# Gates, norms and reciprocal rows moved into the delta steps; operand turns mixed into the first output tile

## The reference

```
h = rms_norm(x); proj = h @ w_in                 # q k v z of the delta net; q k v z of the window attention
dn = gated_deltanet_bidir(...)                   # forward and backward, chunks of 64 tokens, 4 heads of 128
dn = rms_norm(dn, dn_out_norm_w) * silu(dn_z)    # norm over each head's 128 values
sw = windowed_gqa_with_sinks(...) * silu(sw_z)   # 8 query heads of 64, window 128; softmax with a sink
x = x + concat(dn, sw) @ w_out
```

## Time and profile before

| | us |
|---|---|
| median of 3 runs | 2268.99 (2260.82 to 2269.74) |
| profiled execution | 2262.73 |
| its span | 2260.9 |
| TensorE busy in it | 2146.4 (95%) |
| VectorE busy | 1160.1 (51%) |
| ScalarE busy | 728.3 (32%) |
| GpSimd busy | 364.8 (16%) |
| mean granted clock of TensorE | 0.98 |

### The profile page before, as it was taken

The page is one execution under the profiler, slowest core; times in us unless marked ns, Lnnn a source line. Parts: engine busy times, 40 slices in busy tenths (PEclk is TensorE's granted clock), DMA queues, the critical chain, the costliest instruction groups (busy, mean ns, idle before and its releaser), DMA issues. The chain is left out here.

```text
span 2260.9 us, 33793 instructions
## 1 busy us (share of the span) xinstructions
PE 2146.4 (95%) x14358; PEld 1652.8 (73%) x14386; DVE 1160.1 (51%) x1716; ACT 728.3 (32%) x1272; POOL 364.8 (16%) x298
## 2 busy tenths in 40 slices
PE   7999998899987999999997898999999999999998
PEld 6888875677665777876764555778888878878887
DVE  6773326666765866644424665464433433442443
ACT  4223314333332352222224664353312222221221
POOL 3000004212324641111201221350000000000000
PEclk9999998999997999999998999999999999999999
DMA  5113321000004648311214002221111111111112
GB/s 211 47 47 102 92 89 68 2 2 2 2 2 187 203 147 311 126 39 56 76 47 173 1 1 94 79 71 47 44 50 56 41 45 56 47 40 54 47 33 98
DMA packets 185961, 165.81 MB, mean 73 GB/s; under 512 B 13440, under 2 KB 163796, under 8 KB 185684
## 3 DMA queue, kind: packets, MB, share of 16 engines
q1 hardware_dynamic: 180046, 145.18, 20.2%
q0 software_dynamic: 4784, 17.83, 2.0%
q10 hardware_dynamic: 982, 0.65, 0.1%
HBM read 136.90 MB, written 26.74 MB: 72 GB/s over the span
## 5 line engine op out<-in xcount | busy, mean ns | idle before, releaser
L250 PE MATMUL mix_acc<-mix_hi,w_hi 128*128 128x512 f32 x1040 | 415.8, 400 | 0.0
L252 PE MATMUL mix_acc<-mix_hi,w_lo 128*128 128x512 f32 x1040 | 409.9, 394 | 0.0
L251 PE MATMUL mix_acc<-m_lo,w_hi 128*128 128x512 f32 x1040 | 409.4, 394 | 0.0
L230 ACT ACTIVATE w_hi<-w_stage 128x1024 fp32r<-128x1024 f32 x154 | 162.6, 1056 | 457.7 <-PE mix_acc L252 249.1
L238 DVE TENSOR_TENSOR w_lo<-w_stage,w_hi 128x1024 fp32r<-128x1024 f32 x154 | 193.1, 1254 | 110.5 <-ACT w_hi L230 110.5
L3127 DVE SCALAR_TENSOR_TENSOR hidden<-mix_acc,hidden_conv,hidden 128x1023 f32<-128x1023 f32 x88 | 112.8, 1282 | 263.3 <-ACT hidden L3076 261.7
L250 PEld LDWEIGHTS mix_acc<-mix_hi,w_hi 128*128 128x128 f32 x1040 | 195.6, 188 | 52.2 <-issue 8.2
L252 PEld LDWEIGHTS mix_acc<-mix_hi,w_lo 128*128 128x128 f32 x1040 | 195.7, 188 | 45.9
L251 PEld LDWEIGHTS mix_acc<-m_lo,w_hi 128*128 128x128 f32 x1040 | 195.9, 188 | 43.4
L250 PE MATMUL acc<-h_hi,w_hi 128*128 128x512 f32 x400 | 156.8, 392 | 0.9 <-issue 0.9
L252 PE MATMUL acc<-h_hi,w_lo 128*128 128x512 f32 x400 | 155.8, 390 | 0.0
(11 more groups left out here) (359 smaller groups left out, 3741.4 us busy)
## 6 DMA issues: line engine op xcount, KB each, us to landing
w_stage<-in_w_in SPq DMA_DIRECT2D x48, 512.0 KB, 4.3
w_stage<-in_w_up SPq DMA_DIRECT2D x44, 512.0 KB, 3.7
w_stage<-in_w_out SPq DMA_DIRECT2D x32, 512.0 KB, 4.0
w_ada<-in_w_ada SPq DMA_DIRECT2D x32, 512.0 KB, 4.8
spill<-y_tok POOLq DMA_DIRECT2D x21, 512.0 KB, 5.1
m_resid<-resid_spill SPq DMA_DIRECT2D x2, 4096.0 KB, 16.2
conv_in<-in_w_ada SPq DMA_DIRECT2D x16, 512.0 KB, 6.0
conv_in<-spill SPq DMA_DIRECT2D x3, 2048.0 KB, 12.6
```

Of the source, the lines that this page charges most:

```text
L230: nc.scalar.activation(w_hi[:, slot], w_stage[:, slot], ACT.Copy).then_inc(w_hi_ready, 1)
L250: nc.tensor.matmul(acc[:, h, :], w_hi[:, slot, k, :], hi[:, k, tok], start=k == 0, stop=False)
L251: nc.tensor.matmul(acc[:, h, :], w_hi[:, slot, k, :], lo[:, k, tok], start=False, stop=False)
L252: mm = nc.tensor.matmul(acc[:, h, :], w_lo[:, slot, k, :], hi[:, k, tok], start=False, stop=k == kts - 1)
```

## The change

1. In the delta block SyncE loads the attention's gates one block of 128 rows at a time into the queries' place, once the block's scores are made; GpSimd multiplies them into `y_ch` in steps 7, 10, 13 and 15. Only the delta net's gates are loaded at the block's end, in two halves of the tokens.
2. Tiles 3 and 4 of the delta net are complete in step 11, tiles 2 and 5 in 13, tiles 1 and 6 in 15. Their squares (ACT, level 3) and sums (DVE, level 4) stand in that step, root (ACT, level 1) and scaling (DVE, levels 2 and 3) in the next.
3. In step 16 TensorE turns `rcp` at level 3 and ScalarE copies the rows.
4. In the first output projection only tile 0 is normed ahead of the products and tile 7 beside them, by GpSimd's scaling at step 1. The head's roots share one tile.
5. In both projections five units are turned first; units 5, 6 and 7 are turned ahead of the first tile's operands 1, 2 and 3.

```
+                for b in range(4):
+                    sp.wait_ge(s_sc, TT * b + TT)
+                    sp.wait_ge(s_wconst, 48 + 16 * b)
+                    sp.dma_start(qk[:, b, :], scratch(SP_SWZ + b)).then_inc(s_wconst, 16)
...
-                for i, first, signal in ((1, SP_SWZ, s_wconst), (0, SP_Z, s_zl)):
-                    sp.dma_start(conv_in[:, 4 * i:4 * i + 4, :],
+                for h, signal in enumerate((s_zl, s_qk)):
+                    cols = slice(h * HALF, (h + 1) * HALF)
+                    sp.dma_start(conv_in[:, 0:4, cols],
...
+        COMPLETE = {11: (3, 4), 13: (2, 5), 15: (1, 6)}
+        GATED_AT = {7: 0, 10: 1, 13: 2, 15: 3}
...
+                def gated(b):
+
+                    pool.wait_ge(s_wconst, 64 + 16 * b)
+                    pool.wait_ge(s_oc, TT * b + TT)
+                    nc.gpsimd.tensor_tensor(y_ch[:, b, :], y_ch[:, b, :], qk[:, b, :], ALU.mult).then_inc(mix_yn, 1)
...
+                        if s == NCH and lv == 3:
+                            pe.wait_ge(s_den, 4)
+                            for i in range(TT):
+                                mm = nc.tensor.transpose(scb[0:SW_HEADS, i // 4, i % 4 * P:(i % 4 + 1) * P], rcp[:, i, :],
+                                                         ident)
+                            mm.then_inc(s_mod, 1)
...
+                        if s - 1 in COMPLETE and lv == 1:
+                            roots(s - 1)
+                        if s in COMPLETE and lv == 3:
+                            squares(s)
+                        if s == NCH and lv == 3:
+                            copy_rows()
...
+                        if s in COMPLETE and lv == 4:
+                            out_sums(s)
+                        if s - 1 in COMPLETE and lv in (2, 3):
+                            outs_scaled(s - 1, lv - 2)
                         if 0 < s < NCH and lv == 4:
                             advance(s - 1, 0)
...
-            EARLY = 0 if windowed else 3
+            EARLY, TURNED_FIRST = 0 if windowed else 3, 5
...
+                for g in range(EARLY, TURNED_FIRST):
                     turn_unit(pe, g)
+
+                def first_ready(u):
+
+                    if TURNED_FIRST <= u + TURNED_FIRST - 1 < KT:
+                        turn_unit(pe, u + TURNED_FIRST - 1)
+                    pe.wait_ge(mix_lo, r * STEPS + u + 1)
...
+                for g in range(0 if windowed else EARLY - 1, KT):
+                    if windowed and g == 4:
+                        dve.wait_ge(*gates_loaded)
                     operand(dve, g)
-                for g in range(4 if windowed else EARLY - 1, KT):
-                    operand(dve, g)
+                    if windowed and g == 0:
+                        out_sum(0, 7)
+                    if windowed and g == 1:
+                        dve.wait_ge(mix_ors, 4)
+                        out_normed(nc.vector.tensor_tensor, 0)
```

More of the change, by code:

```diff
@@ L1346, in in_gap, with squares, roots, copy_rows @@
                         copy_out(u)
+                def squares(s):
+                    n, _ = completed(s)
+                    act.wait_ge(s_o, 2 * s - 2)
+                    act.wait_ge(mix_oss, 2 * n)
+                    act.wait_ge(mix_yn, 1)
+                    for j, i in enumerate(COMPLETE[s]):
+                        nc.scalar.activation(out_squares_of[:, j, :], o_dn[:, i, :], ACT.Square).then_inc(mix_osq, 1)
+                def roots(s):
+                    n, tiles = completed(s)
+                    act.wait_ge(mix_oss, 2 * n + 2)
+                    nc.scalar.activation(out_rs1[:, tiles, :], out_ss1[:, tiles, :], ACT.Ln, bias=eps[:, 0:1], scale=1.0 / P
+                                         ).then_inc(mix_ln, 1)
+                    act.wait_ge(mix_ln, n + 1)
+                    nc.scalar.activation(out_rs1[:, tiles, :], out_rs1[:, tiles, :], ACT.Exp, scale=-0.5
+                                         ).then_inc(mix_ors, 1)
+                def copy_rows():
+                    act.wait_ge(s_mod, 1)
+                    act.wait_ge(s_kssum, NCH)
+                    nc.scalar.activation(head_rows1, scb[0:SW_HEADS, :, :].rearrange("p a n -> p (a n)"), ACT.Copy
+                                         ).then_inc(s_rcp, 1)
                 decay_exp(0)
@@ L1735, in sync @@
                             load_ada(sp, q)
[L1737 to L1741, removed]
             def operand_lo(pool, g):
@@ L1772, in pool_part @@
                     h, j = s // KT, s % KT
-                    if s == 0 and windowed:
-                        gated(pool, 1)
-                    if s == 3 and windowed:
-                        pool.wait_ge(mix_ors, r * 2 + 2)
-                        for i in range(4, TT):
-                            out_normed(pool, nc.gpsimd.tensor_tensor, i)
+                    if s == 1 and windowed:
+                        pool.wait_ge(mix_ors, 5)
+                        out_normed(nc.gpsimd.tensor_tensor, TT - 1)
                     for g in SECOND_AT.get(s - 1, ()):
@@ L1797, in turn_unit @@
                 if k < 4:
-                    pe.wait_ge(mix_on, r * TT + 4 * h + 4)
+                    pe.wait_ge(mix_on, 7 + h if windowed else TT + 4 * h + 4)
                     for i in range(4):
@@ L1819, in pe_part @@
                     turn_unit(pe, g)
-                for i in range(TT):
-                    mm = nc.tensor.transpose(acc[(c0 + 1) % 2][0:SW_HEADS, i // 4, i % 4 * P:(i % 4 + 1) * P], rcp[:, i, :],
-                                             ident)
-                mm.then_inc(s_mod, 1)
-                for g in range(EARLY, KT):
+                if not windowed:
+                    for i in range(TT):
+                        mm = nc.tensor.transpose(acc[(c0 + 1) % 2][0:SW_HEADS, i // 4, i % 4 * P:(i % 4 + 1) * P],
+                                                 rcp[:, i, :], ident)
+                    mm.then_inc(s_mod, 1)
+                for g in range(EARLY, TURNED_FIRST):
                     turn_unit(pe, g)
+                def first_ready(u):
+                    if TURNED_FIRST <= u + TURNED_FIRST - 1 < KT:
+                        turn_unit(pe, u + TURNED_FIRST - 1)
+                    pe.wait_ge(mix_lo, r * STEPS + u + 1)
                 for s in range(STEPS):
@@ L2011, in dve_part @@
                     split_lo(dve, c + 2, c % 2)
-                    if windowed and s < 4:
-                        out_sum(dve, 4 + s)
+                    if windowed and s == 0:
+                        out_sum(dve, TT - 1, TT)
+                    if windowed and s == 3:
+                        dve.wait_ge(s_qk, 48)
                     for g in SECOND_AT.get(s, ()):
```

126 lines of the change are left out of this document (68 added, 58 removed).

## The result

The changed kernel takes 2274.54 us, median of 10 runs (2272.62 to 2279.53). Runs of the kernel before beside them give 2266.71 us (10 runs, 2260.52 to 2269.74). The ratio is 1.0047, 95% interval 1.0037 to 1.0057: slower by some 0.5%. It is not the quotient of the two medians, which is 1.0035 (+7.8 us). The forecast was 2266 us and the range ended at 2274. (The 10 runs put the kernel before 2.3 us under the median of 3 that the forecast started from, so the miss is larger than the two times say: -3.3 us was forecast, +7.8 came by the medians and some +10.7 by the ratio.)

The account below looks back on a forecast made before the run. TensorE, busy 95% of the span, was taken as the bound, so only its waits and low-clock stretches could give time back. 3.3 + 1.1 - 5.7 - 2.0 = -3.3 us; from the median 2268.99, 2266 us; range 2255 to 2274.

Parts of the forecast that it names:

- The gate products: GpSimd's four products in delta steps 7, 10, 13, 15, about 2.5 us each: hidden, 0; at most 3.6 us in all.
- rival 3: Delta steps: VectorE's 1.25 us behind level 4 idles TensorE, the clock falls, +9 in three steps; 2275 us, chance 0.13.
- all four cases: The forecast of 2266 us and the three rivals' times: 2273, 2260.5 and 2275 us.
- Sums behind level 4: VectorE's pair of sums in steps 11, 13, 15: +1.25, +0.85, +1.2, together +3.3 us, bounds 1.3 and 4.5.
- Scalings and roots at 0: Steps 12, 14, 16: roots and two scalings, the scalings in VectorE's idle time at levels 2 and 3; 0, up to 0.4 us.
- Tail: Step 16: transposes of the reciprocals delay the output sum, two scalings precede the last adds; +1.1 us, bounds 0.3 and 2.3.
- First output projection: Boundary to first tile's end: fewer units ahead, turns alternating with matmuls; -5.7 us, between -6.5 and -2.1.
- Second output projection: Units 5 to 7 alternate with the first tile's matmuls: -4.0 at full clock, +1.5 at 0.50; -2.0 us taken.
- Rival 1: Both output projections: the mixed tile keeps the low clock, -2.1 and +1.5; sum +3.8, 2273 us, chance 0.20.
- the two pieces that were left alone: Step 2, and the stretch from the first projection's first hand-over to the second projection: forecast 0 each.
- The chance of 0.05 for slower: Chance that the whole kernel comes out slower by some 0.5% (11.3 us) or more; 0.85 was given to no change.

Follow-up runs that it names:

- one SBUF tensor: The changed kernel with the negated maximum made by two one-column VectorE instructions, the sink read as a scalar per partition: 2262.3 us, ratio 1.0004.
- fillers with the hold left standing: The changed kernel with six filling matmuls on TensorE at level 2 of steps 7 and 13: 2265.07 us, ratio 1.0003.
- the pieces: The changed kernel with each gate product issued as four GpSimd instructions of 256 columns at the same place: 2264.92 us, ratio 1.0013.
- the move: The changed kernel with two gate products one step later, in steps 8 and 14 instead of 7 and 13: 2260.63 us, ratio 0.9994.
- the last kernel: The kernel before, none of the change, with three filler matmuls at level 1 of odd steps from 3 on: 2262.25 us, ratio 0.9991.
- Three filler matmuls per odd step: Level 1 fillers from step 3, added to the changed kernel with products in steps 8 and 14, sums at levels 2 and 3, second projection turned first: 0.9965.

## Why the prediction was wrong

**The gate products (the step that failed).** The prediction took 0 for all four and at most 0.9 us each, "since the product comes behind the value scaling, when VectorE reads one input from PSUM or transposes". It had the mechanism, an instruction with two SBUF inputs held while GpSimd works, and then didn't find such an instruction beside the product: the negated maximum, 0.16 us long and easily passed over in a timeline. It read the 1.31 us instead of 0.42 as a stretching and took the 0.9 us difference for a bound. It is a wait to the end of GpSimd's instruction, so the bound is that instruction's length, 2.34 us, however small the held one is: 1.64 us measured, 0.70 with pieces, gone with one SBUF tensor. The trace of the kernel before had shown it. In step 4 the negated maximum stood beside GpSimd's scaling of keys and took 0.85 us, up to 449.75, the scaling ending at 449.73:

```profile
448.70 1.03 POOL L966 TENSOR_TENSOR k_dec<-kv_tok,scales 64x512 f32<-64x512 f32 x1
448.90 0.85 DVE L1513 SCALAR_TENSOR_TENSOR max_neg<-row_max,sink_neg 128x2 f32<-128x2 f32 x1
```

Ten negated maxima of the kernel before took 0.33 to 0.85 us in this way. Putting the product right behind the value and key scaling put it where the next maximum falls. The Trainium skill's GPSIMD Engine Reference (section 1, Specifications) names the condition, two SBUF inputs, and the trace agrees; it was cited and then not carried through each VectorE instruction in the product's 2.3 us. In step 10 no negated maximum stands beside the product, and the step grew by 0.06 us; in step 15 the sums explain all.

**The clock in the delta steps (rival 3, with another trigger).** Rival 3 gave 2275 us and 2274.54 was measured, a match by luck (the range was said to take in all four cases and ended 1 us short of this one). By its own mechanism it is wrong: the sums behind level 4 never dropped the clock alone. In step 11 they cost 0.98 us at a clock of 1.00, and with the hold gone the loss went though the sums stayed. The trigger was the hold's pause of 1.45 us, priced nowhere. That hold and clock together make the loss is shown by the medians: fillers with the hold left standing (1.0003), the pieces (1.0013), the move (0.9994) and one SBUF tensor (1.0004) each give back most of it. For a single step the pause causes the fall as a tendency and no more: the clock was low for over 5 us in 7 of the 8 steps 7 and 13 with a full hold and the fillers absent, in 1 of the 4 with a hold of 0.70 to 0.88 us, and in 1 of the 14 without any (the last kernel, the one before with fillers, has none in either step and isn't in the table). One step had the pause and no fall, one the fall and no hold. A fall costs some 4.4 us (27.00 less 22.55), not the 3 that rival 3 took.

**Sums behind level 4:** +1.25, +0.85 and +1.2 forecast. Taking them away gave 0.97 (step 11) and 1.18 (step 15); in step 13 the hold hides it (the clock differs). Right.

**Scalings and roots at 0:** steps 12 and 14 differ by -0.02 and +0.06 us. Right.

**Tail:** +1.1 forecast, +0.5 measured from the scaling of the queries to the boundary, within its bounds, but the sum was another. The terms came larger, 1.6 us (the output sum 0.42 later, the last adds another 1.2), and the clock took 1.1 off again: the value product took 1.09 us instead of 1.97, the one ahead of it 1.70 instead of 1.95. The roots, taken at 0, stand ahead of `v_new` on ScalarE and end the output sum's wait.

**First output projection:** -5.7 forecast, -5.92 measured; first matmul and hand-over within 0.3 us of the values named, the transfer too (14.8 us against 14.5). But the credit given to the mixing was wrong: with all units turned first the tile comes as early. GpSimd's last low half ends TensorE's last wait in either order.

**Second output projection:** -2.0 was taken as the middle of -4.0 and +1.5, and both ends exist: 14.57 to 14.73 us in four profiles of the mixed order, 19.13 to 20.72 in four others, against 18.12 before. The mean of the eight is 17.3, that of the four turned first in versions of the change 17.1. So on average the mixing gives nothing. What sorts these times is the clock, which the prediction ran together with the order:

| at 0.50 in the piece, us | mixed | turned first |
|---|---|---|
| 0 | 14.57, 14.57, 14.61, 14.73 | |
| 3.4 | | 15.75 |
| 6.8 | | 17.09, 17.32 |
| 10.2 | 19.13, 19.17 | 18.12, 18.13 |
| 13.7 | 20.70, 20.72 | |

With 10.2 us at 0.50 the mixed order is 1.0 us slower, and the 6 us between best and worst go with the clock. The forecast took -4.0 for what the mixing gives when the clock stays full; but it is mostly the full clock itself that shortens the piece, and with 3.4 us at 0.50 the old order already takes 15.75. No run shows the old order at full clock throughout. Rival 1's claim, that the mixture keeps a low clock low, is borne out in two profiles of eight (13.7 us against 10.2); in the first projection the clock rose, against it.

**The sum.** With 5.9 us more in step 7, 5.0 more in step 13 and +2.6 instead of -2.0, the forecast of -3.3 becomes +12.2; the two pieces that were left alone, -4.1 and +2.7, make it +10.8, where +10.3 was seen. The chance of 0.05 for slower rested on bounds for the products that were too narrow.

## What to carry to other kernels

Before GpSimd gets a long SBUF instruction, list every VectorE instruction that can start within it and has two SBUF tensors as inputs: in these traces each waited for its end, however small it was, and all that was queued behind waited too. Look in the trace that you have for a small instruction that is long in some places: the price stands there. Read one input as a scalar per partition, cut the long instruction, or move it where the maxima don't stand. Price a pause of TensorE by what it can do to the clock (here 4 to 5 us), and judge a change of a few us in such a kernel by several profiles, not by one.

## What was not expected of the hardware

- The hold ends with GpSimd's instruction (659.78 and 659.76, 520.80 and 520.79). In the traces of all 13 kernels with the two tensors, 139 negated maxima start inside a GpSimd instruction, 0.2 us or more before its end, and every one ends 0.01 to 0.02 us behind it. A larger instruction waits and then still has work: the 128x256 one of 1.31 us ended 0.28 us behind GpSimd's store (619.54 and 619.26).
- The same step with the same pause can keep or lose the clock: 22.55 or 27.00 us. Steps that no edit of the first eleven kernels but the fillers touches moved too: step 2 between 28.63 and 32.92 us, step 5 between 20.46 and 23.57. What decides it wasn't found.
- Three filler matmuls per odd step cost 0.75 us each step (21.08 to 21.84) and still did not slow the kernel: 0.9965 with them, 0.9968 without, 0.9991 on the kernel before. That they gain anything is not shown.
